# Token-major x of a Mamba-2 mixer: TensorE transposes replaced by VectorE block transposes and a DRAM round trip

## What is computed

```python
xbc = jax.nn.silu(causal_dwconv(xbc, conv_w, conv_b))       # 4 taps along the tokens
xs = xbc[..., :D_INNER]   # 4 groups x 8 heads x 64; then B and C, 128 states per group
xdt = x * dtc[..., None]                                     # chunks of 128 tokens
cb = jnp.einsum("bclgn,bcsgn->bcgls", cc, bc)
y_diag = jnp.einsum("bcgls,bcgrls,bcsgrp->bclgrp", cb, decay, xdt)
states = jnp.einsum("bclgn,bcgrl,bclgrp->bcgrpn", bc, decay_to_end, xdt)
y_off = jnp.einsum("bclgn,bcgrpn,bcgrl->bclgrp", cc, prev, jnp.exp(a_cs))
y = y_diag + y_off + d_skip * xs;   y = y * silu(z);   group-wise RMSNorm;   y @ w_out
```

## Time and profile before

| | us |
|---|---|
| median of 3 runs (1106.43 to 1106.49) | 1106.47 |
| time of the profiled execution | 1106.54 |
| its span, first to last instruction | 1104.7 |
| PE busy | 1092.8 |
| DVE / ACT / POOL busy | 577.3 / 474.2 / 610.8 |

### The profile page before, as it was taken

The page is one execution under the profiler, slowest core; times in us unless marked ns, Lnnn a source line. Parts: engine busy times, 40 slices in busy tenths (PEclk is TensorE's granted clock), DMA queues, the critical chain, the costliest instruction groups (busy, mean ns, idle before and its releaser), DMA issues.

```text
span 1104.7 us, 15384 instructions
## 1 busy us (share of the span) xinstructions
PE 1092.8 (99%) x5168; PEld 899.8 (81%) x5168; DVE 577.3 (52%) x644; ACT 474.2 (43%) x816; POOL 610.8 (55%) x460
## 2 busy tenths in 40 slices
PE   9999999999999999999999999999999999999997
PEld 7788888888888788888887888888888888888886
DVE  5665421455432384676777866666664124554123
ACT  7433222233333338458595785343332222333332
POOL 3866544444566635537466376656665444445653
PEclk9999999999999999999999999999999999999999
DMA  7223232222222225333334233222222222333232
GB/s 286 79 99 105 86 103 97 96 95 95 96 95 95 96 77 152 123 112 124 117 104 143 105 125 106 96 95 96 95 95 96 95 95 95 97 99 101 93 104 77
DMA packets 40085, 117.05 MB, mean 106 GB/s; under 512 B 4080, under 2 KB 11888, under 8 KB 40048
## 3 DMA queue, kind: packets, MB, share of 16 engines
q1 hardware_dynamic: 39616, 115.83, 31.3%
q10 hardware_dynamic: 432, 0.73, 0.2%
HBM read 114.32 MB, written 2.23 MB: 105 GB/s over the span
## 4 chain that ended last, share of the span: by engine, by line
PE 93%; ACT 2%; DVE 1%; POOL 1%; issue 1%; DMA 1%; ACTq 0%; DVEq 0%; POOLq 0%
PE bank L857 30%; PE bank L859 29%; PE bank L858 29%; PE bank L1048 1%; PE bank L1057 1%; DMA params<-params 1%; ACT m L634 1%; PE bank L898 1%; PE bank L1007 0%; ACT w_hi L445 0%; POOL w_lo L729 0%; POOL residual L756 0%; PE bank L878 0%; PE bank L1025 0%; ACT y_accumulated L609 0%
## 5 line engine op out<-in xcount | busy, mean ns | idle before, releaser
L729 POOL TENSOR_TENSOR w_lo<-w_raw,w_hi 128x512 fp32r<-128x512 f32 x372 | 497.5, 1343 | 442.5 <-ACT w_hi L445 429.9
L445 ACT ACTIVATE w_hi<-w_raw 128x512 fp32r<-128x512 f32 x372 | 230.5, 626 | 383.0 <-PE bank L859 373.5
L857 PE MATMUL bank<-x_hi,w_hi 128*128 128x512 f32 x848 | 331.9, 391 | 1.8 <-DVE x_lo L1159 1.5
L859 PE MATMUL bank<-x_hi,w_lo 128*128 128x512 f32 x848 | 330.2, 389 | 0.0
L858 PE MATMUL bank<-x_lo,w_hi 128*128 128x512 f32 x848 | 330.1, 389 | 0.0
L857 PE MATMUL bank<-act_hi,w_hi 128*128 128x512 f32 (+1 forms) x656 | 252.9, 386 | 0.0
L859 PE MATMUL bank<-act_hi,w_lo 128*128 128x512 f32 (+1 forms) x656 | 251.8, 384 | 0.0
L858 PE MATMUL bank<-act_lo,w_hi 128*128 128x512 f32 (+1 forms) x656 | 251.8, 384 | 0.0
L857 PEld LDWEIGHTS bank<-x_hi,w_hi 128*128 128x128 f32 x848 | 159.2, 188 | 37.5 <-issue 2.8
L859 PEld LDWEIGHTS bank<-x_hi,w_lo 128*128 128x128 f32 x848 | 159.2, 188 | 33.1
L858 PEld LDWEIGHTS bank<-x_lo,w_hi 128*128 128x128 f32 x848 | 159.3, 188 | 32.6
(11 more groups left out here) (161 smaller groups left out, 725.8 us busy)
## 6 DMA issues: line engine op xcount, KB each, us to landing
w_raw<-weights SPq DMA_DIRECT2D x186, 512.0 KB, 3.3
m<-acs_scratch SPq DMA_DIRECT2D x16, 512.0 KB, 4.4
decay_in<-eacs_scratch SPq DMA_DIRECT2D x24, 128.0 KB, 3.8
x_token<-x_tok SPq DMA_DIRECT2D x4, 512.0 KB, 6.4
residual<-xt SPq DMA_DIRECT2D x8, 256.0 KB, 10.1
out_first<-scaled_residual SPq DMA_DIRECT2D x4, 256.0 KB, 2.4
out_second<-output_rows SPq DMA_DIRECT2D x4, 256.0 KB, 2.7
pooling_matrices<-pooling ACTq DMA_DIRECT2D x2, 288.0 KB, 5.2
```

The source lines that it names most:

```text
L445: act.activation(whi[:, c % 2, part], raw[:, c % 2, part], ACT.Copy).then_inc(hi_ready, 1)
L729: pool.tensor_tensor(wlo[:, c % 2, part], raw[:, c % 2, part], whi_f[:, c % 2, part], ALU.subtract).then_inc(lo_ready, 1)
L857: pe.matmul(out, wh, xh, start=start, stop=False)
L859: return pe.matmul(out, wl, xh, start=False, stop=stop)
```

## The change

x goes token-major without PE. When group g+1's x is convolved and activated, DVE transposes each 32x32 block of it (`transpose_blocks`) into the not yet used `yx` tiles of that group, SP writes them to a DRAM scratch (`write_blocks`, four DMAs with runs of 128 elements), and reads them back with tokens on partitions (`read_tokens`, one DMA with runs of 512 elements). DVE's `token_x` then reads SBUF instead of PSUM, in two instructions per chunk. So that x is ready early, the convolution order becomes x, x, x, x, B, C. `silu_x` moves from t = 0 to t = 8 of the group before, `skip` from t = 0 to t = 3 (it overwrites the landed rows), the fourth `token_x` from t = 3 to the end of t = 2. The state update's three-part product is the same in both kernels. The group-order of the weights on the host follows the new convolution order.

```diff
         def conv_out(n):
             g, q = divmod(n, CONVS)
-            return bf[:, :] if q == 0 else cf[:, g % 2, :] if q == 1 else xact[:, q - 2, :]
+            return xact[:, q, :] if q < GT else bf[:, :] if q == GT else cf[:, g % 2, :]
...
+            def write_blocks(g):
+                sp.wait_ge(xt_blocks, g + 1)
+                blocks = x_blocks(g)
+                for a in range(P // Q):
+                    sp.dma_start(x_dram[g, :, :, a, :].rearrange("n q f -> q n f"),
+                                 blocks[Q * a:Q * a + Q, :, :]).then_inc(xt_written, 16)
+            def read_tokens(g):
+                sp.wait_ge(xt_written, 16 * (P // Q) * (g + 1))
+                sp.dma_start(yx[:, GT * g:GT * g + GT, :],
+                             x_dram[g].rearrange("(c b) q a f -> (b q) c (a f)", c=CHUNKS)
+                             ).then_inc(xt_landed, 16)
...
             for u in range(5):
                 load_ahead(u)
+            write_blocks(0)
             sp.wait_ge(acsf_ready, 1)
...
             load_ahead(5)
+            read_tokens(0)
             sp.wait_ge(scratch, 2 * GROUPS * 16)
...
+                    if t == 8 and g + 1 < GROUPS:
+                        write_blocks(g + 1)
+                    if t == 9 and g + 1 < GROUPS:
+                        read_tokens(g + 1)
...
# ACT
+                if u == 4:
+                    silu_x(0)
                 first_tap(u)
...
+                    if not ends and t == 8:
+                        silu_x(g + 1)
                     ahead(u, 0)
                     if t == 0:
                         silu_b_c(g)
-                        silu_x(g)
...
-                    if t == 0:
+                    if t == 3:
                         skip(g)
...
# PE
             def token_major(g):
                 pe.wait_ge(bc_act, 2 * g + 2)
                 if g:
-                    pe.wait_ge(xdt_ready, 4 * g)
+                    pe.wait_ge(bt_lo_ready, g)
...
-                pe.wait_ge(x_act, g + 1)
-                if g == 0:
-                    pe.wait_ge(acsf_ready, 1)
-                else:
-                    pe.wait_ge(y_add, 4 * g)
-                    pe.wait_ge(y_dec, 3 * g)
-                    pe.wait_ge(state_ready, 3 * g)
-                for c in range(CHUNKS - 1):
-                    token_x(g, c)
...
             def chunk(g, c):
                 pe.wait_ge(m_ready, 4 * g + c + 1)
                 pe.wait_ge(xdt_ready, 4 * g + c + 1)
...
-                    if t == T_LATE_TOKEN:
-                        pe.wait_ge(bt_lo_ready, g + 1)
-                        token_x(g, CHUNKS - 1)
...
# DVE
+            def transpose_blocks(g):
+                dve.wait_ge(x_act, g + 1)
+                blocks = x_blocks(g)
+                for i in range(GT):
+                    last = dve.transpose(blocks[:, :, Q * i:Q * i + Q],
+                                         xact[:, i, :].rearrange("p (n j) -> p n j", j=Q))
+                last.then_inc(xt_blocks, 1)
...
             def token_x(g, c):
-                dve.wait_ge(x_mm, 4 * g + c + 1)
-                dve.tensor_tensor(by_head(xdt[:, c, :]), by_head(XT_BANK[c][:, :]),
+                dve.wait_ge(xt_landed, 16 * (g + 1))
...
+                for half in range(2):
+                    last = dve.tensor_tensor(out[:, half], landed[:, half],
+                                             dt[:, half].unsqueeze(2).unsqueeze(3).to_broadcast([P, GT, 2, Q]),
+                                             ALU.mult)
...
                         conv_scale(CONVS * (g + 1) + t - GT)
+                        if t == 8:
+                            transpose_blocks(g + 1)
...
                         conv_taps(CONVS * (g + 1) + t - GT)
```

More of the change, by code:

```diff
@@ L56 @@
 TIMES_CB_IN = {4: 1, 6: 2, 8: 3}
-T_TOKEN, T_LATE_TOKEN = 1, 2
+T_TOKEN = 1
+Q = 32
 T_STAT, T_NORM = 4, 7
@@ L256, in build @@
         cb_mm = sem("cb_product")
-        x_mm = sem("x_transposed")
+        xt_blocks = sem("x_blocks_transposed")
+        xt_written = sem("x_blocks_written")
+        xt_landed = sem("x_token_major_landed")
         xdt_ready = sem("x_dt_ready")
@@ L323, in lo_source, with x_blocks @@
             return lo_ready, 2 * c + half + 1 + 2 * r
+        def x_blocks(g):
+            return yx[:, GT * g:GT * g + GT, :].rearrange("p i t -> p (i t)").rearrange("p (n f) -> p n f", f=GT * Q)
         def conv_out(n):
             g, q = divmod(n, CONVS)
[L328 removed]
+            return xact[:, q, :] if q < GT else bf[:, :] if q == GT else cf[:, g % 2, :]
         block = ctx.enter_context(nc.Block())
@@ L574, in first_tap, with silu_x @@
                                ).then_inc(tap_ready, 1)
+            def silu_x(g):
+                act.wait_ge(acc_drained, A_SSM + conv_slot(CONVS * g + GT - 1) + 1)
+                act.activation(xact[:, :, :], xact[:, :, :], ACT.Silu).then_inc(x_act, 1)
             for u in range(CONVS):
@@ L595, in silu_b_c @@
             def silu_b_c(g):
-                for q in range(2):
+                for q in range(GT, CONVS):
                     act.wait_ge(acc_drained, A_SSM + conv_slot(CONVS * g + q) + 1)
                     act.activation(conv_out(CONVS * g + q), conv_out(CONVS * g + q), ACT.Silu).then_inc(bc_act, 1)
-            def silu_x(g):
-                act.wait_ge(acc_drained, A_SSM + conv_slot(CONVS * g + CONVS - 1) + 1)
-                act.activation(xact[:, :, :], xact[:, :, :], ACT.Silu).then_inc(x_act, 1)
             def skip(g):
-                act.wait_ge(x_act, g + 1)
+                act.wait_ge(xdt_ready, 4 * g + 4)
                 for i in range(GT):
@@ L1002, in _ @@
                     cumulate()
-            def token_x(g, c):
-                for i in range(GT):
-                    last = pe.transpose(XT_BANK[c][:, P * i:P * i + P], xact[:, i, P * c:P * c + P], ident)
-                last.then_inc(x_mm, 1)
             def token_major(g):
@@ L1044, in chunk @@
                 pe.wait_ge(xdt_ready, 4 * g + c + 1)
-                if c:
+                if g == 0 and c == 0:
+                    pe.wait_ge(acsf_ready, 1)
+                else:
                     pe.wait_ge(y_add, 4 * g + c)
@@ L1053, in chunk @@
                     pe.wait_ge(state_ready, 3 * g + c)
-                    if c > 1:
+                    if g or c > 1:
                         pe.wait_ge(y_dec, 3 * g + c - 1)
@@ L1062, in chunk @@
                     pe.wait_ge(bt_lo_ready, g + 1)
-                    if c == 0:
-                        pe.wait_ge(xdt_ready, 4 * g + 3)
+                    if g and c == 0:
+                        pe.wait_ge(state_ready, 3 * g)
                     three(b_st[:, :], bt_hi[:, c, :], bt_lo[:, c, :], dec_hi[:, :], dec_lo[:, :], True, True
@@ L1323, in _ @@
                 conv_scale(u)
+                if u == 4:
+                    transpose_blocks(0)
                 conv_taps(u)
@@ L1345, in token_x @@
             def token_x(g, c):
-                dve.wait_ge(x_mm, 4 * g + c + 1)
-                dve.tensor_tensor(by_head(xdt[:, c, :]), by_head(XT_BANK[c][:, :]),
-                                  of_group(dt_t[:, :, :].rearrange("p c h -> p (c h)"), c, g, HD), ALU.mult
-                                  ).then_inc(xdt_ready, 1)
+                dve.wait_ge(xt_landed, 16 * (g + 1))
+                if g and c == 0:
+                    dve.wait_ge(yd_ready, 4 * g)
+                    dve.wait_ge(dec_ready, 3 * g)
+                out = xdt[:, c, :].rearrange("p (i h a j) -> p h i a j", h=2, a=2, j=Q)
+                landed = yx[:, GT * g + c, :].rearrange("p (h a i j) -> p h i a j", h=2, a=2, j=Q)
+                dt = dt_t[:, c, HPG * g:HPG * g + HPG].rearrange("p (i h) -> p h i", h=2)
+                for half in range(2):
+                    last = dve.tensor_tensor(out[:, half], landed[:, half],
+                                             dt[:, half].unsqueeze(2).unsqueeze(3).to_broadcast([P, GT, 2, Q]),
+                                             ALU.mult)
+                last.then_inc(xdt_ready, 1)
             def b_token_lo(g):
@@ L1504, in _ @@
                         decay_times_cb(g, 0)
+                        token_x(g, 3)
                     if t == T_NORM and g:
@@ L1591, in conv_cols @@
     def conv_cols(g):
-        return np.r_[b0 - x0 + g * P:b0 - x0 + (g + 1) * P, c0 - x0 + g * P:c0 - x0 + (g + 1) * P,
-                     g * gw:(g + 1) * gw]
+        return np.r_[g * gw:(g + 1) * gw, b0 - x0 + g * P:b0 - x0 + (g + 1) * P,
+                     c0 - x0 + g * P:c0 - x0 + (g + 1) * P]
     ssm = [units(w_in[:, x0 + conv_cols(0)])]
```

4 lines of the change are left out of this document (1 added, 3 removed).

## The result

The changed kernel takes 1113.92 us (median of 4 runs, 1112.87 to 1114.56) where the kernel before takes 1106.48 (4 runs, 1106.43 to 1106.64): a ratio of 1.0066, 95% interval 1.0049 to 1.0084. It is 7.4 us slower; 2.5 us faster was forecast, and the time lies outside the stated range of 1099.5 to 1111. The profiled execution took 1114.36, of which 1112.6 are span, with a mean granted clock of 0.993 (0.998 before).

The account below looks back on a forecast made before the run. PE was taken as the bound (busy 1092.8 of 1104.7 us). Gains for groups 0 to 3, 0.8 + 1.67 + (0.4 - 0.8) + 0.4 = 2.5 us, took 1106.5 to 1104.0 us; range 1099.5 to 1111.

Parts of the forecast that it names:

- That is the whole gain that is to be had: PE's removed transposes: 1.67 us a group, 6.7 us over four groups, as the most that could be gained.
- keep its 1.67: Group 1: m for chunk 0 comes 2.8 us early, so the group keeps its full 1.67 us.
- buys nothing: ACT at t = 0: lighter by 1.90 and 2.56 us, without gain because ACT waits for the gate.
- Six halves with one meeting: DVE's six half products before m: 1.8 us plus 1.1 for one meeting with POOL, done at 574.5.
- the forecast 576.7: Chunk 0 of groups 2 and 3: DVE's product m ends at 576.7, PE asks at 575.6 and waits 1.1 us.
- The rival that I gave 0.23: DVE becomes the bound through dear transposes (1111 to 1118) or three more POOL meetings in groups 2 and 3 (about 5 us).
- Everything that DVE does after the scaling of t = 8 comes ... 1.6 later: DVE at t = 8: four transposes take 2.4 us, 0.85 of it hidden under a wait for ACT.
- Group 0: First group: m at 441.2, PE asks at 440.6; 0.9 us lost, 0.8 kept, range 1.67 kept to 1 lost.
- one of my signs of being wrong: The forecast is wrong if the read of x appears as a releaser of DVE; no size given.
- The round trip: DMA writes and read of x in groups 1 to 3: lands near 568, hidden by some 2 us.
- Chunk 2 of group 2: Chain to m now has ACT's skip before the rounding: 0.8 us put on PE, between 0 and 2.

Follow-up runs that it names:

- e9: Kernel before with PE's 16 transposes of x a group left out and nothing in their place: 1104.30 us.
- e4: Kernel before with only the new conv order (x first, B and C last) and SiLU of x at t = 8: 1111.14 us.
- e5: e4 with SiLU of x at t = 8 moved behind the roundings, just ahead of the first tap: 1108.81 us.
- e13: e5 with POOL waiting for DVE's gate of the group before, ahead of the low part of the weights of t = 1: 1105.28 us.
- e2: Changed kernel with dt copied into a PSUM bank, so the half products have one SBUF input instead of two: 1112.01 us.
- e10: e5 with four DVE transposes at t = 8 as work on top, their result overwritten: 1114.09 us.
- e1: Changed kernel with 12 filler matmuls on PE in the stall ahead of chunk 0 of groups 2 and 3: 1112.70 us.
- e11: e10 with the DMA round trip (writes and read) as work on top, read by nobody: 1112.63 us.
- e3: Changed kernel with x landing in a free part of the z buffer, so the skip is back at t = 0 in groups 0 to 2: 1113.99 us.
- e6: Changed kernel with SiLU of x at t = 8 moved behind the roundings: 1113.13 us.
- e17: e6 with dt in PSUM, POOL waiting for DVE's gate, ACT's exponential before the squares, and two of POOL's three square sums later: 1106.33 us.
- e14: e6 with POOL waiting for DVE's gate ahead of the second half of t = 1: 1109.92 us.

## Why the prediction was wrong

**"That is the whole gain that is to be had", 6.7 us.** The 1.67 us a group are right as PE's time, and groups 0 and 1 showed them (chunk 0 of group 1 at 506.79 against 509.53). Group 1, however, did not "keep its 1.67": waits of 0.91 and 1.05 at its chunks 2 and 3, which my sum did not have, used up the whole lead. As a gain the 6.7 were never there: without the transposes and with nothing in their place the kernel wins 2.1 us (e9). I had seen 1.0 us of slack at chunk 0 of group 2 and a wait of 0.98 at chunk 2, and used them only for those two places. They were the sign that DVE, ACT and POOL were level with PE over the whole of groups 1 to 3, so that all of PE's time beyond the first bit would come back as waits for m.

**The new order, costed at nothing.** My sum has no term for it; of ACT's lighter load at t = 0 I wrote that it "buys nothing". It costs 4.7 us by itself (e4), 2.3 by the place of the SiLU at t = 8 (e5). The rest is the gate: with ACT lighter, the weights are rounded sooner, POOL comes to them sooner, and the low part falls on DVE's gate (e13 takes 3.5 us off e5 by keeping the two apart). So a lighter ACT did not buy nothing, it cost time. In the changed kernel the gate ended at 570.5 instead of the forecast 569.2, and ACT's exponential with it at 576.4 instead of 575.1.

**Six halves with one meeting, 1.8 + 1.1 = 2.9 us.** They took 5.12 in group 2. This is the term that was mis-sized. The price of a meeting was about right, 3.04 / 3 = 1.0 us over e2's 2.08; the count was wrong, three of the six instead of one in each of groups 1 to 3. In group 0, where one of the six met POOL, they took 2.95. I had DVE through at 574.5, ahead of ACT; it was through at 577.7, 1.4 us behind ACT. With ACT's 1.3 us above and a product m·cb that took 1.23 instead of 1.54, this makes the difference between m at the forecast 576.7 and at 578.97. The rival that I gave 0.23 had this in its second half, the products meeting POOL again and again, and there it has come true, if with two more meetings and not three; its first half, a dear transpose, has not. e2 shows that it is the meeting. The Trainium skill (SBUF — State Buffer, section Who interferes with whom) says that a DVE instruction with two SBUF inputs contends with a GpSimd instruction that reads SBUF, and that one with at most one does not, outside the modes in which DVE uses two ports. By that rule each product beside a busy POOL had to be priced as a meeting, and e2's 2.08 against 5.12 agrees with it.

**"Everything that DVE does after the scaling of t = 8 comes ... 1.6 later"** was right in its parts: 2.48 us for four transposes (0.60 each after the first; I took 0.61), 0.85 hidden. In e10 the gate began 1.3 us later for it, and PE's waits grew by 1.1 and 0.9 in groups 2 and 3, close to the 1.3 that I let come of it. What I did not price is what a longer stall does to the clock: e10 is 3.7 to 5.3 us above e5, of which the waits are 2.0.

**The clock** is in no term. Stalls of 3.3 us took TensorE to 1.2 GHz. In the changed kernel this is worth 1.2 us between medians (e1), less than the windows suggest, since in group 2 the lost time would have been spent waiting for m of chunk 2.

**Group 0** was about right: m was ready at 440.31 (441.2 forecast), PE's chunk 0 began at 440.36, and the low weights behind it cost a wait of 0.55. DVE's wait of 2.75 for the read of x there was one of my signs of being wrong, and it came, but it cost PE nothing: it lay beside ACT's wait of 3.44 for m's values, and DVE then waited another 2.18 for ACT.

**The round trip** was right in groups 1 to 3: no wait of DVE for it, and e11 finds no price. The margin is thin in group 1: in e2 DVE comes to it sooner and waits 1.87. SP's writes took 0.76 us each (median) instead of 1.2.

**Chunk 2 of group 2:** 0.8 foreseen, 0.30 measured. The waits at chunk 3 (1.05 and 1.06) were not foreseen; e3 clears the skip of them, and e6, where they are gone, gives them to the SiLU.

What makes up the 7.4 us, as steps from kernel to kernel, between medians: the order with its SiLU 4.7 (e4), of which 2.3 come back in e5; transposes 5.3 on top of e5, about half of it clock; the round trip nothing that the clock's spread lets one see (e11 is 1.5 below e10); then, from e11 to e6, products and skip on one side and PE's saved time on the other, 0.5 in sum; and 0.8 from e6 to the changed kernel. The single steps are rough, since executions of one kernel lie up to 2.8 us apart (e2), the slower ones at a lower clock.

What stays open: why the clock falls in some executions and not in others after an equal stall, how much of the step from e11 to e6 is the products and how much the skip, and what PE's transposes are worth once DVE's gate and POOL are kept apart (e9's edit on top of e13 was not run). Whether the change has a form that beats e13 was not found: the best of its forms, e17, is level with the kernel before, and e13 keeps PE's transposes.

## What to carry to other kernels

An engine at 99% is not alone at the bound when the others' results arrive a microsecond ahead of it. Take the work out with nothing in its place first, and read what waits appear, before pricing a replacement. Look at the stretch that decides, not at the share of the whole: DVE was 52% busy and had 5 us idle in the 34 that mattered. And when an edit moves work on one engine, follow who starts sooner by it: DVE with two SBUF inputs and POOL lose time where they meet, and making one wait can be the faster order.

## What the runs showed of the hardware

- A DVE instruction with two SBUF inputs beside POOL's subtraction: four gate products take 2.48 us alone (e13) and 4.68 beside it (e5), while POOL's two pieces go from 2.55 to 3.53. Six 256-element products with two inputs in SBUF take 5.12, three of them beside POOL; with one input in PSUM they take 2.08 (e2).
- The granted clock fell after a stall of 2.04 us in group 3 of e2 (chunk 0 behind it took 1.39 us instead of 1.09; 0.51 from 651 to 657), and not after 1.67 in e4. After the same 2.5 us it fell in e10 and held in e11. In one execution of e14 it fell after 2.39 us (0.50 from 579 to 582) and held after 2.42 (1.00 from 648 to 652). The Trainium skill (TensorE: Matmul & The Clock Gate, Part 1) says that the number of slow matmuls at the start of one kernel varies from run to run; here it is so in the middle of one: the five runs of e10 lie in two clusters 1.7 us apart.
- A block transpose of 128x512 fp32 from SBUF to SBUF takes DVE 0.67 us, the same as its other 512-element instructions with one SBUF input. The Trainium skill's figure for bf16, 311 ns for 128x128 (VectorE: DVE Perf Modes, The three transpose paths), would have made four of these blocks 1.2 us; the measurement is a little over half of that estimate.
- The write of 256 KB in runs of 512 bytes lands 4.1 us after its issue, the read of 1 MB 7.3 us.
